# Who requests the light experts' weights in a mixture-of-experts loop: ScalarE beside its silu instead of SyncE

## What is computed

```python
def run_block(args):
    xb, e = args
    hdn = jax.nn.silu(xb @ w_gate[e]) * (xb @ w_up[e])
    return hdn @ w_down[e]
```

## Time and profile before

| | us |
|---|---|
| median of 3 runs | 1865.59 |
| lowest and highest | 1862.32, 1867.0 |
| the profiled execution, its own time | 1859.31 |
| its span in the profile | 1857.5 |
| `experts`: first gather issued, last light product begun | 1121.0 to 1757.3 |
| first transfer of `combine` issued | 1777.5 |

### The profile page before, as it was taken

One profiled execution on the slowest core, in us unless ns is written; L12 is line 12 of the kernel. 1 busy time (PEld: TensorE's weight loads), 2 busy tenths in 40 slices (PEclk: granted clock), 3 DMA queues, 4 the chain that ended last, 5 costly groups with the idle time before them and its releaser, 6 DMA issues. The chain is left out here.

```text
span 1857.5 us, 20999 instructions
## 1 busy us (share of the span) xinstructions
PE 1498.5 (81%) x7352; PEld 839.3 (45%) x7353; DVE 626.0 (34%) x1073; ACT 355.4 (19%) x585; POOL 112.1 (6%) x110
## 2 busy tenths in 40 slices
PE   5999979777765989999899515999999999999700
PEld 1555534336761865666455412444444444444300
DVE  1222144435885323433567440110101010101058
ACT  2111022212222333333211001111111111111122
POOL 0000000000002000000000031111111111111000
PEclk8999989977996999999999657999999999999955
DMA  9100021050006020000411008969888989999653
GB/s 366 47 23 11 1 35 45 11 182 1 0 13 222 1 91 0 0 0 0 145 68 61 32 1 300 384 218 387 316 319 314 394 316 392 353 385 395 250 229 133
DMA packets 145972, 298.90 MB, mean 161 GB/s; under 512 B 25596, under 2 KB 35848, under 8 KB 144915
## 3 DMA queue, kind: packets, MB, share of 16 engines
q1 hardware_dynamic: 137412, 280.73, 41.1%
q0 software_dynamic: 8384, 16.81, 2.6%
q10 hardware_dynamic: 146, 0.98, 0.2%
HBM read 282.85 MB, written 25.73 MB: 166 GB/s over the span
## 5 line engine op out<-in xcount | busy, mean ns | idle before, releaser
L377 PE MATMUL ps<-w_in_tok,uT_tiles 128*128 128x512 f32 (+2 forms) x512 | 191.4, 535 | 1.2 <-ACT uT_tiles L298 1.2
L1794 PE MATMUL ps<-w_gate_sb,x_slotsT 128*128 x320 | 145.2, 607 | 9.4 <-issue 7.6
L1824 PE MATMUL ps<-w_down_sb,hidT 128*128 x320 | 142.1, 597 | 11.1 <-DVE hidT L1882 11.1
L1794 PE MATMUL ps<-w_up_sb,x_slotsT 128*128 x320 | 140.6, 592 | 0.0
L377 PEld LDWEIGHTS ps<-w_in_tok,uT_tiles 128*128 128x128 f32 x512 | 97.7, 192 | 89.8 <-issue 61.1
L458 PE MATMUL ps<-uT,w_qk 128*128 128x512 f32 x256 | 111.6, 599 | 10.9 <-DMA w_qk<-in_w_in 10.9
L1877 DVE TENSOR_TENSOR hid<-silu_g,ps 128x512 f32<-128x512 f32 x20 | 13.8, 688 | 298.2 <-PE ps L1794 298.2
L1393 PE MATMUL ps<-w_out,hT 128*128 128x512 f32 x256 | 114.2, 600 | 0.0
L1794 PEld LDWEIGHTS ps<-w_gate_sb,x_slotsT 128*128 128x128 f32 x320 | 60.1, 193 | 87.2 <-issue 87.2
L1794 PEld LDWEIGHTS ps<-w_up_sb,x_slotsT 128*128 128x128 f32 x320 | 60.8, 190 | 76.5 <-issue 76.5
L1824 PEld LDWEIGHTS ps<-w_down_sb,hidT 128*128 128x128 f32 x320 | 59.1, 190 | 79.7 <-issue 79.7
(11 more groups left out here) (372 smaller groups left out, 1980.4 us busy)
## 6 DMA issues: line engine op xcount, KB each, us to landing
light_gate_sb<-in_w_gate SPq DMA_DIRECT2D x20, 2048.0 KB
light_up_sb<-in_w_up SPq DMA_DIRECT2D x20, 2048.0 KB
light_down_sb<-in_w_down SPq DMA_DIRECT2D x20, 2048.0 KB, 12.3
w_gate_sb<-in_w_gate SPq DMA_DIRECT2D x12, 2048.0 KB
w_up_sb<-in_w_up SPq DMA_DIRECT2D x12, 2048.0 KB, 14.8
w_down_sb<-in_w_down SPq DMA_DIRECT2D x12, 2048.0 KB
uT<-in_w_ada SPq DMA_DIRECT2D x8, 2048.0 KB, 9.9
y_pair<-expert_rows SPq DMA_DIRECT2D x8, 1024.0 KB, 7.1
```

Of the source, the lines that this page charges most:

```text
L377: mm = nc.tensor.matmul(ps[:, 2 + g, 0:n], uTt[:, j, k, :], wt[:, k, c0:c0 + n], start=k == 0, stop=k == KD - 1)
L1794: m = m_.matmul(ps[:, bank, :], xT[:, k, :], wt[:, bass.ds(buf, 1), k, :].rearrange("p a f -> p (a f)"), start=k == 0, stop=k == KD - 1)
L1824: m = m_.matmul(ps[:, 5 + half, :], hT[:, k, :], wd[:, bass.ds(buf, 1), k, half * 512:half * 512 + 512].rearrange("p a f -> p (a f)"), sta ...
```

## The change

The table gets one column more, so that row 6 can be read at b+1. SP keeps the heavy weights alone. ACT requests the light gate and up weights of iteration 0 before its loop, those of b+1 right behind its silu of the light product of b, and the light down weights of b at the start of iteration b, after a wait for the light down product of b-1. Only the requests and their place move; the transfers, their sizes and their buffers stay.

```diff
-        self.tbl = self.sb("block_table", [1, 7, NB], I32, ctx=ctx)
+        self.tbl = self.sb("block_table", [1, 7, NB + 1], I32, ctx=ctx)
...
-                lk(v.tensor_copy(self.tbl[:], tf[:]))
+                lk(v.tensor_copy(self.tbl[:, :, 0:NB], tf[:]))
...
-                        le = entry(sp, 6, b, E - 1)
-                        sp.wait_ge(s_lG, b + 1)
-                        sp.dma_start(lwg[:], wg_d[bass.ds(le, 1)].rearrange("a p k f -> p (a k) f")).then_inc(s_lgu, 16)
-                        sp.dma_start(lwu[:], wu_d[bass.ds(le, 1)].rearrange("a p k f -> p (a k) f")).then_inc(s_lgu, 16)
-                        sp.wait_ge(s_lY, b + 1)
-                        sp.dma_start(lwd[:], wd_d[bass.ds(le, 1)].rearrange("a p k f -> p (a k) f")).then_inc(s_ld, 16)
...
+                def light_gate_up(e):
+                    act.dma_start(lwg[:], wg_d[bass.ds(e, 1)].rearrange("a p k f -> p (a k) f")).then_inc(s_lgu, 16)
+                    act.dma_start(lwu[:], wu_d[bass.ds(e, 1)].rearrange("a p k f -> p (a k) f")).then_inc(s_lgu, 16)
+
+                light_gate_up(entry(act, 6, 0, E - 1))
                 act.wait_ge(s_xt, 1)
...
                     with act.If(b < n):
+                        act.wait_ge(s_lY, b + 1)
+                        act.dma_start(lwd[:], wd_d[bass.ds(entry(act, 6, b, E - 1), 1)].rearrange("a p k f -> p (a k) f")).then_inc(s_ld, 16)
                         act.wait_ge(s_G, b + 2)
...
                         a.activation(sgl[64:P, :], ps[0:64, 7, 0:HF], ACT.Silu).then_inc(s_lsg, 1)
+                        with act.If(b + 1 < n):
+                            light_gate_up(entry(act, 6, b + 1, E - 1))
                         act.wait_ge(s_lxt, b + 2)
```

## The result

The change costs time: 1867.49 us in the median of 20 runs against 1860.01 of 20 runs of the kernel before, ratio 1.0036 with a 95% interval of 1.0023 to 1.0049. The difference is +7.5 us where +7.8 was forecast; the interval of the ratio is +4.3 to +9.1 us. The profiled execution took 1869.62 us, its span 1867.8. The next fences show its waits, its timeline and its queues; SP's list of requests is six lines shorter, so L1806 of before is L1800 now, L1794 is L1788 and L1767 is L1761.

A forecast was written before the change was run, and what follows sets the result against it. The prediction took PE to bound the loop, with the DMA engines a close second limit. Its terms, 1.5 + 1.5 + 2 + 3 + 2 - 2.2 = +7.8 us, on 1865.6 gave 1873.4 us, range 1861 to 1883.

The forecast's parts named there:

- start: Iteration 0: light packets delay heavy gate weights 5.35 us, the later light product's wait goes; net +1.5 us (0 to +2.3).
- block 14: Light pair shares the bus with three heavy experts requested in iterations 12 to 14; late 0 to 2.1 us, taken +2.
- block 2: SP running ahead requests the third heavy expert in iteration 1; light product of iteration 2 late 0 to 2.8, taken +1.5 us.
- block 15: Light pair queues behind iteration 14's light down weights at half rate; late +1 to +5 us, taken +3.
- block 18: Behind two heavy experts in a row, light pair late as in iteration 14; taken +2 us.
- waits that go: PE's earlier waits of 1.04 us in iteration 15 and 1.17 in iteration 19 disappear; -2.2 us.
- The requests themselves: ACT's added loads, branch and requests fit the gaps in its schedule and delay no product; 0 us on PE.
- Sharing, packet for packet: SP's and ACT's full queues move equal numbers of packets, the total staying at 393 GB/s.
- asked for 1.2 us later, window 25.6 instead of 26.8: Every iteration: ACT requests the light pair 1.2 us later than SP did, shrinking its window from 26.8 to 25.6 us.
- the starved queue: Rival, slower, chance 0.04: SP's backlog goes wholly first, some 10 us in each of three or four places; 1900 us.
- The light loads: Rival, same time, chance 0.27: light loads keep up in blocks 2, 14, 15 and 18; 1864.9 us.
- The spread pays: Rival, faster, chance 0.13: SP's earlier heavy requests relieve dense iterations and all waits go; -8.8 us, 1856.8 us.

The follow-up runs named there:

- the first experiment: Changed kernel with ACT's first light pair requested only behind its copy of the turned rows, so behind POOL's first gather; ratio 1.0044, loop 680.40 us.
- the ninth experiment: Changed kernel with iteration 0's six loads requested by SP alone in order of need, the rest in two queues; ratio 1.0042, loop 680.94 us.
- the seventh experiment: Changed kernel with the light pair requested behind ACT's copy of the turned light rows instead of its light silu; ratio 1.0031, loop 676.18 us.
- the third experiment: Changed kernel with SP requesting heavy down weights only once the next iteration's light pair has landed; ratio 1.0011, loop 670.84 us.
- the second experiment: Changed kernel with SP requesting block b's heavy expert no earlier than the end of iteration b-1's heavy gate product; ratio 1.0028, loop 680.46 us.

## Why the prediction was right, step by step

The sign and the mechanism held (two full queues share, so the light pair comes late where heavy weights stand beside it), and 1867.49 lies in the range of 1861 to 1883. That the size came out so close, +7.5 for +7.8, is in good part luck. The forecast stood on a median before of 1865.6 from 3 runs; over 20 it is 1860.01, so the 1873.4 forecast is 5.9 us above the time measured, and only the difference fits. And the terms were further off than their sum: the start and block 14 cost 3.8 us more than forecast, blocks 2, 15 and 18 together 5.3 less. The forecast's border of 0.3% lies inside the interval of 1.0023 to 1.0049, so whether the change costs more or less than that stays open. The loop's +6.3 us, from the table:

| term | forecast | measured | |
|---|---|---|---|
| start | +1.5 (0 to +2.3) | +3.9 | outside its own range |
| block 2 | +1.5 (0 to 2.8) | 0 | at its lower end |
| block 14 | +2 (0 to 2.1) | +3.4 | outside |
| block 15 | +3 (1 to 5) | +0.7 | below |
| block 18 | +2 (0 to 2.1) | +0.5 | inside |
| waits that go | -2.2 | -2.2 | |
| sum | +7.8 | +6.3 | |

*The requests themselves, 0 on PE.* Right. PE waits once for a copy of ACT, 1.1 us at the start (L1766 for L1847), and that falls within its wait for the gate weights; the longest of ACT's 60 requests took 2.26 us. The tail of the loop did not move: 22.25 us behind ACT's last copy PE's sequencer still lets the last stage go, as in the earlier trace rows.

```profile
1787.76 1.28 ACT L1949 ACT_TABLE_LOAD   x1 [22.25 <-PEq L1667]
```

*Sharing, packet for packet.* Right, and shown for the two hardware queues themselves: 700 to 700, 416 to 418 with 1.55 to 0.85 MB. The light down loads, 12.3 us in the median before, take 15.1 (the line of ACT's own requests for them, minimum, median, longest):

```profile
DMA to landing us min/median/max: 7.9/15.1/27.1
```

*Start.* The mis-sized term. I delayed the heavy gate weights by the light packets that pass beside them, 5.35 us. From the gather's issue to the first gate product 11.3 us became 20.0, 8.7 more. The first experiment gives it all back, so it is ACT's head start. PE stands 7.14 us for the gate weights when the rows have long been turned, so the gather, itself 4.1 us later, is not what holds the gate product. The queues show where the 8.7 us go. After, from SP's request to 1130.9, then from 1130.9 to 1142.9:

```profile
q10 hardware_dynamic: 629, 1.29, 83.6%
q0 software_dynamic: 61, 0.25, 14.7%
q1 hardware_dynamic: 4, 0.01, 0.5%
```

```profile
q10 hardware_dynamic: 1031, 2.08, 46.3%
q1 hardware_dynamic: 1020, 2.07, 46.0%
q0 software_dynamic: 295, 0.52, 11.6%
```

Before, from 1124.9 to 1130.9:

```profile
q1 hardware_dynamic: 1010, 2.05, 95.1%
q0 software_dynamic: 59, 0.04, 2.0%
```

The gate weights take 12.0 us to pass instead of 6.0, with one light packet for each of theirs, as forecast, and with 0.52 MB of POOL's, which I had left out. And they begin late: requested at 1126.44, 4 of their packets are through by 1130.9, while the pair and then the gather pass; before, 22 were through 2.3 us behind the request. I had ACT's head start of 3.1 us in the sum of bytes, but gave it no delay. Which of the two in front, pair or gather, holds back the first packets was not separated. Of the 3.2 us that the gate product starts later than forecast, 0.85 came back, as it ran 8.86 us instead of 9.71. The wait of 4.88 with its half clock went, as forecast, and left +3.9.

*Blocks 2, 14, 15 and 18.* Where heavy and light collide was right, except block 2, on time in the changed kernel, which is 3.9 us late by then: with the start repaired its wait is there (3.61 us in the ninth experiment). How the lateness is spread was wrong. My step "asked for 1.2 us later, window 25.6 instead of 26.8" carries no weight: the seventh experiment asks 1.2 us later again and the wait is the same. As I read it, the sum of bytes ahead of the pair decides. As to 15, I let SP's queue be full until about 1615 in every case, but each wait of PE gives the queues as much time to catch up; this too is a reading. Three figures of the working don't follow from its own rows: SP's four loads more put ACT's first request at 1118.9 and not 1119.5 (the trace has it 3.26 us ahead of SP's, so near the latter), 39.0 MB in place of 38.0 are 2.4 us late and not 2.8, and 16 us ahead of a pair with 1.3 us of slack are 14.7 us late and not some 10, so the starved queue was priced too low.

*The rivals.* The light loads did not keep up. "The spread pays" was half true: running ahead does relieve the dense iterations once the down weights are held (the third experiment, no wait from 1 to 19), and taking it away costs 4.9 us more, half clock included (the second); what it needs is an order that the second queue takes away. The rule of the Trainium skill that I weighed (DMA: Bandwidth & Descriptors, section "Issuing engines are not separate DMA queues") says that requests from several engines interleave on the same DMA engines. This trace agrees, 700 packets beside 700. That such a change is then worth nothing was my conclusion from it, and it was the wrong one: interleaving takes away the order in which the transfers were asked for, and the loop grew by 6.3 us.

## What to carry to other kernels

Where transfers and compute both fill a loop, write down when each load is needed and ask for them in that order in one queue; the order is then kept for free. A second queue shared packet for packet here (700 to 700), so it hands half the bus to whatever stands in it, needed or not, and packets of twice the size took two thirds (1.55 MB beside 0.85). Before moving a request earlier, list everything that is under way at that moment on every queue, gathers of another engine included, and who waits for it.

## What the runs showed that I had not expected

**The clock behind a short wait.** In iteration 14 PE waited 3.39 us in the changed kernel and kept 2.4 GHz. After 4.12 us in the first experiment it had 1.2 GHz for a while, and the step was 6.67 us, 2.5 more than the wait. After 3.27 us in the seventh it fell too, 0.4 us after work had begun; the stretch from 1599.2 to 1602.4 has 0.54:

```profile
1595.50:1599.20 3.70, 0.43 (x8) 0.29 (x12) 0.00 (x0) 1.01 (x1) 1.05 (x1) 1.00 1.03 399
1599.20:1602.40 3.20, 3.20 (x37) 1.63 (x33) 0.00 (x0) 0.00 (x0) 0.00 (x0) 0.54 1.03 394
```

The changed kernel behind its 3.39 us:

```profile
1597.50:1600.50 3.00, 2.98 (x56) 1.85 (x60) 0.00 (x0) 0.00 (x0) 0.00 (x0) 1.00 1.03 393
```

Shorter waits do either too. In the second experiment PE waits 2.90 us in iteration 18 and 2.17 in 19; the stretches behind the two:

```profile
1714.00:1717.00 3.00, 2.94 (x56) 1.83 (x60) 0.00 (x0) 0.00 (x0) 0.00 (x0) 1.00 1.04 390
1747.00:1750.00 3.00, 3.00 (x32) 1.60 (x36) 0.00 (x0) 0.00 (x0) 0.00 (x0) 0.53 0.64 261
```

The longer cost itself, 3.0 us; the shorter 3.9 (a step of 2.65, with the 1.2 that the kernel before loses there). So a wait of 2 to 4 us costs between itself and 1.8 times itself, and its length alone doesn't tell which.

**A load asked for just ahead of a gather.** The gather of 0.52 MB takes 4.5 us from issue to use where no weights were asked for before it, and 8.2 to 8.7 where any hardware queue was 1 to 1.7 us ahead, whichever engine had asked (ACT in the changed kernel, SP in the ninth experiment).

**Drift ahead of the loop.** The same code ahead of the loop ended between 1102.1 and 1116.1 us in thirteen profiles, more than any effect studied here on the loop. By the span, the third experiment (1852.9 us) is 4.6 us shorter than the kernel before (1857.5); by the loop it is 1.6 us longer, and its ratio of 1.0011 agrees with the loop.
